# Everything behind the recurrence as two joined programs without barriers, and the feed-forward loops written out

## The reference, cut to what matters

```python
for l in range(DEPTH):
    x = x + 0.5 * swiglu(rmsnorm(x, norm_ffn1[l]), ffn1_w_gate[l], ffn1_w_up[l], ffn1_w_down[l])
    h = rmsnorm(x, norm_mix[l])
    ...                     # l = 0: x + rwkv7_time_mix(h), l = 1: x + nsa_attention(h, shared)
    x = x + 0.5 * swiglu(rmsnorm(x, norm_ffn2[l]), ffn2_w_gate[l], ffn2_w_up[l], ffn2_w_down[l])
    if l == N_A - 1:
        shared = nsa_shared_kv(x, ...)
```

## Time and profile before

| | us |
|---|---|
| median of 3 runs | 2622.4 (2622.07 to 2625.19) |
| the profiled execution | 2623.52 |
| its span, first to last instruction | 2621.7 |
| instructions recorded | 44256 (no time) |
| PE busy | 2379.2 (91%) |
| DVE busy | 1590.1 (61%) |
| ACT busy | 627.0 (24%) |
| POOL busy | 575.7 (22%) |
| PEld, weight loads beside the matmuls | 1927.0 (74%) |

### The profile page before, as it was taken

How to read it: one execution, slowest core, us unless ns; L and a number is a source line. 1 busy time by engine, 2 the same in 40 slices (tenths; PEclk the granted TensorE clock), 3 DMA queues, 4 the chain that set the end, 5 groups by cost and what they waited for, 6 DMA issues and landing times. The chain is left out here.

```text
span 2621.7 us, 44256 instructions
## 1 busy us (share of the span) xinstructions
PE 2379.2 (91%) x17560; PEld 1927.0 (74%) x17560; DVE 1590.1 (61%) x2152; ACT 627.0 (24%) x1219; POOL 575.7 (22%) x390
## 2 busy tenths in 40 slices
PE   7999996996888779999998899999949998999998
PEld 6888874774666568888876788887638887788887
DVE  6656459964777536555563665656646665665654
ACT  3100012223555511000023210101535552210001
POOL 3212134522222122121220121213121201221213
PEclk9999996997999889999999899999969999999999
DMA  4333321441111023333245333332341102233322
GB/s 132 104 89 104 89 80 53 125 131 49 28 33 26 3 71 106 99 94 99 82 119 159 84 96 97 96 96 81 109 110 38 38 1 65 81 105 88 104 84 69
DMA packets 376085, 217.25 MB, mean 83 GB/s; under 512 B 18896, under 2 KB 359824, under 8 KB 375920
## 3 DMA queue, kind: packets, MB, share of 16 engines
q1 hardware_dynamic: 367792, 199.09, 27.1%
q10 hardware_dynamic: 8128, 15.83, 1.8%
HBM read 199.00 MB, written 15.89 MB: 82 GB/s over the span
## 5 line engine op out<-in xcount | busy, mean ns | idle before, releaser
L143 DVE TENSOR_TENSOR w_lo_ffn<-w_raw,w_hi_ffn 128x1024 fp32r<-128x1024 f32 x272 | 508.8, 1870 | 9.4
L387 POOL TENSOR_TENSOR act_ffn<-gated_ffn,usc_ffn 128x512 f32<-128x512 f32 x88 | 128.2, 1457 | 1007.8 <-ACT gated_ffn L367 1007.8
L367 ACT ACTIVATE gated_ffn<-gsc_ffn 128x512 f32<-128x512 f32 x88 | 55.7, 633 | 1010.2 <-DVE gsc_ffn L292 1010.2
L150 PE MATMUL p_gate_ffn<-hhi_ffn,w_hi_ffn 128*128 128x512 f32 x704 | 278.8, 396 | 7.5 <-DVE hlo_ffn L205 7.5
L292 DVE TENSOR_TENSOR gsc_ffn<-p_gate_ffn,rstd_ffn 128x512 f32<-128x512 f32 x88 | 60.9, 692 | 363.9 <-PE p_up_ffn L152 363.3
L150 PE MATMUL p_up_ffn<-hhi_ffn,w_hi_ffn 128*128 128x512 f32 x704 | 275.1, 391 | 2.9 <-DVE w_lo_ffn L143 2.9
L151 PE MATMUL p_gate_ffn<-hlo_ffn,w_hi_ffn 128*128 128x512 f32 x704 | 277.7, 394 | 0.0
L152 PE MATMUL p_gate_ffn<-hhi_ffn,w_lo_ffn 128*128 128x512 f32 x704 | 277.6, 394 | 0.0
L150 PE MATMUL p_down_ffn<-ahi_ffn,w_hi_ffn 128*128 128x512 f32 x704 | 275.4, 391 | 2.4 <-DVE x_res L303 2.4
L151 PE MATMUL p_up_ffn<-hlo_ffn,w_hi_ffn 128*128 128x512 f32 x704 | 275.0, 391 | 0.0
L152 PE MATMUL p_up_ffn<-hhi_ffn,w_lo_ffn 128*128 128x512 f32 x704 | 274.9, 390 | 0.0
(11 more groups left out here) (351 smaller groups left out, 4312.7 us busy)
## 6 DMA issues: line engine op xcount, KB each, us to landing
w_raw<-in_ffn_w_gate_dram SPq DMA_DIRECT2D x88, 512.0 KB, 3.9
w_raw<-in_ffn_w_up_dram SPq DMA_DIRECT2D x88, 512.0 KB, 3.9
w_raw<-in_ffn_w_down_dram SPq DMA_DIRECT2D x64, 512.0 KB, 3.7
w_raw<-in_ffn_w_down_dram SPq DMA_DIRECT2D x32, 384.0 KB, 3.3
w_raw<-in_rw_w_rkv_dram SPq DMA_DIRECT2D x24, 512.0 KB, 4.2
rkv_scratch<-staged_mix ACTq DMA_DIRECT2D x24, 256.0 KB, 2.4
w_raw<-in_kv_w_dram SPq DMA_DIRECT2D x12, 512.0 KB, 5.0
w_raw<-in_rw_w_o_dram SPq DMA_DIRECT2D x8, 512.0 KB, 4.7
```

The source lines that it names most:

```text
L143: nc.vector.tensor_tensor(lo, raw, fp(hi), ALU.subtract).then_inc(s["w_ready"], 1)
L150: nc.tensor.matmul(out, whi, hi, start=first, stop=False)
L367: nc.scalar.activation(gated[:], gsc[:, j], ACT.Silu).then_inc(s["silu"], 1)
L387: nc.gpsimd.tensor_tensor(act32[:], gated[:], usc[:, j], ALU.mult).then_inc(s["act32"], 1)
```

## The change

Two programs replace the nine stages behind the recurrence, other than attention. `middle` is the output projection of the time mix, the feed-forward behind it, the shared keys and values, the first feed-forward of layer 1, and the queries. `closing` is the output projection of the attention, the last feed-forward, and the transposes of the output. `opening` is the first feed-forward alone, in the same classes. Setup, mixing, recurrence and attention stay as they are, each still a stage.

- A program has one `Region`: one ring with one running count of units, one pair of `hi` and `lo` tiles, one set of eight PSUM banks. Stages become classes (`Add`, `Ffn`, `SharedKv`, `Queries`, `Output`), called one after the other on each engine.
- The norm's tile work moves into the end of the part before: behind each finished tile of x, ACT makes the high part and the square, POOL the sum, DVE the low part. PE sums over partitions inside the first two units, ahead of the sixth k.
- The first two units of a feed-forward, of the keys and values and of the queries are multiplied together, k by k.
- All `Fori` loops of the feed-forward are Python loops.
- In `SharedKv` the compressed part is spread over the units: read-back of the plain units and windows early, its products behind units 8, 9 and 10 and behind the last one, two of them in the middle of the next feed-forward.
- In `Queries` the sums, normalizations and swaps have lists that say behind which unit they stand; two banks each for sums and swaps.
- `Output` transposes each finished tile of x beside the last down units and stores in three parts.

```diff
+    def scalar_tile(self, act, d):
+        core, s, A = self.core, self.s, self.core.nc.scalar.activation
+        if self.ready:
+            act.wait_ge(self.ready[0], self.ready[1] + d)
+        if self.gain is not None:
+            A(self.region.hi[:, d], core.x[:, d], ACT.Copy, scale=self.gain[:, d:d + 1]).then_inc(s["h_hi"], 1)
+        if not self.shared:
+            if d >= 2:
+                act.wait_ge(s["sq_sum"], d - 1)
+            A(core.sq[:, d % 2], core.x[:, d], ACT.Square).then_inc(s["sq"], 1)
...
+class Ffn:
...
+    def vector(self, dve):
...
+        if self.first:
+            region.split(dve, 0)
+            for d in range(ND):
+                self.norm.vector_tile(dve, d)
+            for u in range(1, 4):
+                region.split(dve, u)
+        self.norm.vector_rstd(dve)
...
-                with dve.Fori(0, nf // 2) as i:
+            for i in range(nf // 2):
...
+                V.scalar_tensor_tensor(out=core.x[:, d], in0=bank[:, 4 + d % 2], scalar=0.5, in1=core.x[:, d],
+                                       op0=ALU.mult, op1=ALU.add).then_inc(s["x_done"], 1)
+                if last and d:
+                    self.after.vector_tile(dve, d - 1)
+                region.split(dve, unit + d + 4)
...
+        for f0, nf in self.groups:
+            if f0 == 0:
+                pe.wait_ge(s["gu_free"], 1)
+                for k in range(ND):
+                    pe.wait_ge(self.norm.s["h_lo"], k + 1)
+                    if k == 5:
+                        self.norm.tensor_sum(pe)
                     for j in range(2):
...
+                        if k == 0:
+                            pe.wait_ge(ring["w_ready"], done(unit + j))
+                        mm = three_passes(core, bank[:, 2 * j], j, k, region.hi[:, k], region.lo[:, k], k == 0, k == ND - 1)
...
+                if f0 + nf == NF:
+                    for e in range(2) if d == 2 else [d - 1]:
+                        self.after.tensor_tile(pe, e)
...
+class Queries(Heads):
...
+        self.sums_behind = {2: [0], 3: [1, 2], 4: [3], 5: [4], 6: [5], 7: [6], 8: [7]}
+        self.normal_behind = {3: [0], 4: [1], 5: [2, 3], 6: [4], 7: [5], 8: [6]}
+        self.swaps_behind = {4: [0], 5: [1], 6: [2, 3], 7: [4], 8: [5]}
...
+class SharedKv(Heads):
...
+            if u in (6, 7):
+                self.windows(dve, 0, range(8 * (u - 6), 8 * (u - 5)))
+            if u in (9, 10):
+                self.windows(dve, 1, range(8 * (u - 9), 8 * (u - 8)))
+        for d in range(3):
+            following.vector_tile(dve, d)
+        self.rotate(dve, 3)
+        for d in range(3, ND):
+            following.vector_tile(dve, d)
...
+            if u - 1 in self.rotated:
+                self.head_sums(pe, self.rotated.index(u - 1))
...
+            if u == 8:
+                pe.wait_ge(self.norm.s["ms"], 1)
+                self.turn(pe, 0)
+                self.hidden(pe, 0, 0)
+            if u == 9:
+                pe.wait_ge(c["copied"], 1)
+                self.turn(pe, 1)
+                self.hidden(pe, 0, 1)
+            if u == 10:
+                pe.wait_ge(c["copied"], 2)
+                pe.wait_ge(c["w2"], 32)
+                pe.wait_ge(c["gelu"], NH)
+                for t in range(NH):
+                    mm = T_.matmul(self.p_c[0:C, 0:NB], self.w2[:, 0, t], self.hid[t], start=(t == 0), stop=(t == NH - 1))
...
+        pe.wait_ge(c["raw"], 1)
+        self.turn(pe, 2)
+        self.hidden(pe, 1, 0)
+        self.swap_halves(pe, 3)
+        pe.wait_ge(c["copied"], 3)
+        pe.wait_ge(c["sqc"], 1)
...
+        self.hidden(pe, 1, 1)
+        pe.wait_ge(c["c_ln"], 1)
+        self.turn(pe, 3)
...
+            if u - 1 in self.rotated:
+                self.rate(act, self.rotated.index(u - 1))
+            if u in (8, 9):
+                self.keep_turned(act, u - 8)
+                self.store(act, u - 8)
+            if u == 10:
+                self.activate(act, 0)
...
+        @block.tensor
+        def _(pe):
+            pe.sem_inc(region.ring["w_free"], SLOTS)
+            add.tensor(pe)
+            one_.tensor(pe)
+            shared.tensor(pe)
+            two.tensor(pe, between=shared.tensor_end)
             heads.tensor(pe)
```

More of the change, by code:

```diff
@@ L152, in three_passes @@
     return nc.tensor.matmul(out, wlo, hi, start=False, stop=last)
[L155 to L176, removed]
@@ new lines, in unit, with head_sums @@
+    def unit(self, pe, u):
+        region = self.region
+        pe.wait_ge(region.ring["w_ready"], done(self.base + u))
+        if u >= 4:
+            pe.wait_ge(self.s["xt"], u - 3)
+        for k in range(ND):
+            mm = three_passes(self.core, region.bank[:, u % 4], u % 4, k, region.hi[:, k], region.lo[:, k], k == 0, k == ND - 1)
+        mm.then_inc(region.ring["w_free"], 1)
+    def head_sums(self, pe, r):
+        pe.wait_ge(self.s["sqx"], r + 1)
+        if r >= len(self.p_ss):
+            pe.wait_ge(self.s["ln"], r - len(self.p_ss) + 1)
+        self.core.nc.tensor.matmul(self.p_ss[r % len(self.p_ss)], self.core.head_ones[:], self.sqx[:, r % 2], start=True, stop=True).then_inc(self.s["ss"], 1)
@@ L1664, in _ @@
-            sp.wait_ge(s["w_ready"], done(len(units) - 1))
+            ffn.sync(sp)
+            sp.wait_ge(region.ring["w_ready"], done(len(region.units) - 1))
             load_ahead(sp, core, ahead)
@@ L1671, in _ @@
         @block.tensor
         def _(pe):
-            heads.tensor(pe)
+            pe.sem_inc(region.ring["w_free"], SLOTS)
+            add.tensor(pe)
+            one_.tensor(pe)
+            shared.tensor(pe)
+            two.tensor(pe, between=shared.tensor_end)
+            heads.tensor(pe)
+        @block.sync
+        def _(sp):
+            add.sync(sp)
+            one_.sync(sp)
+            shared.sync(sp, one_, add)
+            two.sync(sp, between=shared.sync_end)
+            heads.sync(sp, two)
+            shared.sync_stored(sp)
+            sp.wait_ge(region.ring["w_ready"], done(len(region.units) - 1))
+            load_ahead(sp, core, ahead)
@@ L1790, in _ @@
[L1790 to L1807 removed]
+            add.scalar(act)
@@ new lines, in program @@
+        with ExitStack() as held:
+            hold = lambda name, shape, dt=F32: held.enter_context(nc.sbuf_tensor(name, shape, dt))
+            lora = {n: hold(f"lora_{n}", [P, c, T]) for n, c in (("wa", 1), ("lg", 2))}
+            mix_project(core, "mix", rkv, lora)
+            with ExitStack() as output:
+                yhi, ylo = (output.enter_context(nc.sbuf_tensor(n, [P, ND, T], F32R)) for n in ("y_hi", "y_lo"))
+                recurrence(core, "rec", rkv, lora, yhi, ylo)
+            middle(core, "b", yhi, ylo, lora, ins["rw_w_o"][0], ffn_in(2, 0), ffn_gain(2, 0), shared, core.vec("kv_norm"),
+                   ffn_in(1, 1), ffn_gain(1, 1), ins["nsa_w_q"][0], ins["nsa_q_norm"][0], queries, core.vec("norm_mix", 1),
+                   first_units(ins["nsa_w_o"][0]))
```

1231 lines of the change are left out of this document (679 added, 552 removed).

## The result

The kernel after takes **2576.61 us** in the median of four runs (2573.63 to 2579.64), the one before 2622.24 of four; the ratio is 0.9824, with a 95% interval of 0.9807 to 0.9841. The forecast was 2562.8, with a range of 2549 to 2586. So 45.6 us were saved where 59.5 were expected: the sign and the range were right, the gain was put three tenths too large.

The account below looks back on a forecast made before the run. PE's pace bounds the feed-forwards, so only boundaries could gain: 9.1 + 9.1 + 27.2 + 17.2 + 4.6 - 7.7 = 59.5 us saved, span 2562.2, forecast 2562.8 us, range 2549 to 2586.

Parts of the forecast that it names:

- Opening: Start of the first feed-forward: unit 2 begins at 46.1 us where it was 38.33, 7.7 us lost, not covered.
- Output projection to feed-forward: Both such joints: other engines' work is covered, no slow start on PE, 11.78 us against 20.91, 9.1 saved each.
- Feed-forward, keys and values, feed-forward: Stretch across the shared keys and values: 112.1 us against 139.3, including a wait and slow start, 27.2 saved.
- The new wait: Behind unit 10 of the keys and values, PE waits 6.3 us for gelu, plus 1.7 of slow start.
- Feed-forward to the end of the queries: From that feed-forward's end to the queries' last store: 70.5 us against 87.7, no wait within, 17.2 saved.
- The barrier to attention stays: Between the queries' last store and attention: the barrier remains, with no change in time counted.
- The end: Behind the last feed-forward: 10.0 us against 14.6, with seven transpose groups among the down units, 4.6 saved.
- Loops written out: Feed-forward loops unrolled: nothing taken, from 0 to some 2 us either way.
- VectorE being late at the joints: Rival: DVE falls behind in the last down units, PE waits 3 to 5 us at four joints; 2578, chance 0.15.
- the missing wait: Rival: PE does not wait for gelu behind unit 10 of the keys and values; 2555 us, chance 0.12.
- the slower pace of written-out units: Rival: unrolled feed-forward units take 0.2333 us a matmul against 0.2267, 45 less saved; 2608, chance 0.06.
- late instructions: Rival: unrolled feed-forwards need about 34 more instruction packets, each a 2.8 us stop, 95 us; 2658, chance 0.04.

Follow-up runs that it names:

- the 73 idle semaphores: Kernel before with 73 unused semaphores added to the queries' stage, so that it closes with 104: 2628.77 us against 2622.96, ratio 1.0025.

## Why the prediction was right in sign and range, and too low by 14 us

- **Opening, 7.7 forecast, 9.5 measured.** The mechanism was right, and both halves of it were shown. The last high tile came earlier than forecast (27.82 for 28.8), yet the last low tile, put at 29.7, came at 32.1: GpSimd's sums slow VectorE's low tiles too (13.24 us for eight), where the forecast slowed only the weights' split. In return the split of unit 1 came when GpSimd was done and took 1.95 us and not 3.95. The forecast's own sum had a slip: 29.7 and 3.95 are 33.6 and not 33.3. TensorE restarted at 34.02. The slow start was put at 1.7 us and took about 2.7 here, twelve steps at 0.43 (34.62 to 39.72); in the other profiles of the same opening it took 1.5 to 3.0, so this part of the miss is chance.
- **Output projection to feed-forward, 9.1 forecast, 5.1 measured, twice: the step that failed.** "Covered, and PE has no slow start" was worked out from tiles and sums alone. The change puts the credit for the gate and up banks, a semaphore increment that costs nothing and waits for nothing, behind the output projection's steps in VectorE's order. It arrives 2.1 us late, and in eleven of fourteen such joints, these two among them, the slow start followed that pause. With the credit moved, the joint takes 11.78 us, the forecast's own figure. Of the 14 us missed, 8.
- **Feed-forward, keys and values, feed-forward: 27.2 forecast, 28.6 measured.** The new wait was where it was said to be, released by the gelu. It was 4.6 us and not 6.3: the table for the Ln was loaded at 1418.02, before the head sum was there, so one load of 1.28 us was off the path. The slow start behind it, eight steps at 0.43, cost about 2.0 against the run with the gelu first, for the 1.7 taken. Another late credit cost 1.0 us at the second feed-forward. TensorE's own work was about 1 us less than the 104.1 summed. The rows show again a load before the Ln and one before the Exp, and the gelu at 1426.47 right behind its load (1425.18 + 1.28). The Trainium skill (ScalarE: Activation LUTs, "Table sets: the hidden batching unit" and "What ACT_TABLE_LOAD costs") has one load for the two, and a drain of some 1.4 us with each load. This trace agrees with neither, and the measurement decides.
- **Feed-forward to the end of the queries, 17.2 and 17.7.** Right.
- **"The barrier to attention stays".** It did, but 4.9 us longer, because a barrier here is priced by how many semaphores its stage owns. Joining stages takes barriers away and makes one that stays dearer. The forecast counted the barriers and not what they do. Shown by the 73 idle semaphores.
- **The end, 4.6 and 6.1.** Both parts were priced too high. The seven groups of transposes cost 2.9 us for 3.2. Behind the last unit (2566.16) 5.6 us pass for the 6.8 summed, most of it because the store of 1 KB pieces was not slower than before: from the end of ScalarE's copy (2568.40) to the end of the span pass 3.4 us, where 3.7 and up to 0.9 were taken.
- **Loops written out, 0.** Right within the noise: the feed-forwards keep their pace, and the run of the loops alone is 2.6 us slower, with an interval that just holds no change.

Together: 1.8 (opening) + 8.0 (credits) + 4.9 (semaphores) - 1.4 - 0.5 - 1.5 (the three that gave more) - 1.8 (all else) is 9.6 before rounding, the difference between 59.5 and 49.9. The other 4.3 to the medians is that one profiled run was 3.0 under its median and the other 1.3 over.

That the time fell inside the range is in part luck. Two mechanisms, the credits and the semaphores, were not in the forecast at all, and 5.2 us of other differences hid a part of them. The upper end was put at 2586 for VectorE being late at the joints, a rival at 2578; 2576.6 lies beside that figure, but that mechanism did not occur.

Of the **rivals**, the missing wait did not happen. DVE late at the joints did not either: TensorE waits for no split at any joint inside the two programs. Nor did the slower pace of written-out units (2230 to 2560 of after: full, clock 1.00), nor late instructions: 140 packets, 21 more where 34 were estimated, and no stop.

```profile
2230.00:2560.00 330.00, 329.41 (x1461) 271.97 (x1460) 191.81 (x184) 28.21 (x45) 58.05 (x41) 1.00 0.31 93
```

## What to carry to other kernels

When two programs are joined, list every instruction of each engine at the seam, the free ones too: a credit, or any other semaphore increment, that used to run at once now stands behind whatever that engine still waits for, and its reader pays the pause and often the slow clock after it. Price a barrier by what it does, here 0.064 us for each semaphore that SyncE clears, before counting the ones that go; joining stages moves that cost into the ones that stay. And an interleaving made for two units that are ready (k by k over both) costs time where only one is, as in the opening; what it gains at the joints no run here shows by itself.

## What the hardware did that was not expected

- Clearing a semaphore at a stage's end took SyncE 0.064 us (4.67 us for 73), and five engines sharing the work took up to 4.4 us off one barrier of 104.
- Behind TensorE's pause of 2.1 us at the first joint came a stretch mostly at the 1.2 GHz level (granted clock 0.57 from 984.70 to 988.70). Such stretches differed in length: seven steps of 0.43 us at the joint, eight behind the gelu, twelve in the opening, and five to twelve in five profiles of the same opening. In three of fourteen joints none came behind the same pause, and none behind the 1.03 us pause of the third credit. With the credit moved, 4.0 us went for a pause of 2.1.
- Beside GpSimd's sums VectorE's low tile took 1.76 us (985.77) or 1.65 on average (13.24 for eight), against 0.74 with GpSimd idle (983.25); a split took 1.9 us alone and 3.95 beside them.
- The recurrence, the same code in all, took between 320.2 and 323.9 us in profiles of the kernel after and its variants. Single edits of a few us are therefore better read at their own place in the trace than in the medians.
